# Where the first modulation of a layer is computed: at the head of the layer, or beside the mixers of the layer before

## The chip, the cores and the metric

The kernel runs on one core of a Trainium2 chip. The metric is the device time of one execution in microseconds (us). Lower is better.

## The reference

One inference step of a two-layer decoder trunk, for 512 prompt tokens and 8 single-token samples with shared weights (520 columns in all, width 1024). Cut to what matters here:

```python
def _block(x, c, st, pos, lb, p):
    mod = silu(c) @ p['ada_w'] + p['ada_b']               # 6 x 1024 per sequence
    sh1, sc1, g1, sh2, sc2, g2 = split(mod, 6)
    h = _rmsnorm(x, p['norm_mix_w']) * (1.0 + sc1) + sh1  # the first modulation
    mix, new_st = _mixer(h, st, pos, lb, p)               # RWKV-7, retention, gated delta, HGRN2, gates, w_out
    x = x + g1 * mix
    h = _rmsnorm(x, p['norm_ffn_w']) * (1.0 + sc2) + sh2
    gu = h @ p['w_gate_up']
    x = x + g2 * ((silu(gu[..., :D_FF]) * gu[..., D_FF:]) @ p['w_down'])
    return x, new_st
# two layers, then y = _rmsnorm(x, final_norm_w)
```

`c` (the conditioning) is the same in both layers and does not depend on x. So `mod` of every layer could be computed at any time; only h needs x.

## The kernel before, in words

Everything lies transposed: features on the 128 partitions (`KT` = 8 tiles), the 520 tokens along the free axis. The program has three parts: a block that loads constants and x and prepares tables, a hardware loop over the two layers (`nc.Fori`, L460), and a last block with the final norm. Between them all engines meet at a barrier, and the loop jumps back at its end. Inside a layer, each engine has its own instruction list, and semaphores tie them together.

**Weights.** They come as tiles of 128 x 1024 (0.5 MB) through a ring of four slots. `loads()` sets the order, SP issues a load as soon as the slot's last user is done (`load_tile`, L548). Since TensorE multiplies here in three parts (high x high, high x low, low x high), each weight tile of a large product is split first: the high part by ScalarE (`round_weights`, L1162) or by GpSimd (L602), the low part by GpSimd in two halves (L605). A large product (`large`, L652) is 48 matmuls of 128 x 260, six for each of eight slices of the input. It writes one of the two banks `gm`, which ScalarE or VectorE must empty before the product after next may start.

**Modulation.** The 48 tiles of `mod` come in twelve groups of four (`ADA_STEP`). A group is two products `ada` (L684, each from two ring tiles, taken by ScalarE at L1148 into a room of the arena) and one `turn` (L699), which turns the result onto the partitions with `PICK`; VectorE adds the bias (`modulation`, L2017). Groups 0 to 3 hold shift and scale of the first norm. Before the change they are the head of each layer: `first_modulation()` (L143).

**The order of a layer.** PE: wait for parameters and squares, sum over features (`feature_sums`, L756), the first modulation (L1074), then the plan. VectorE: squares of x and their sum (L2047 to L2051), modulation, `norm` (L1543), which also scales by 1 + sc. ScalarE: half of the squares, the root (`root_mean_square`, L1150: Ln, then Exp), the copies, its part of the norm.

**The plan** (`plan_layer`, L105) lists mixer stages and tasks. The mixers are HG, RW, GD, RT, one after the other, each a chain of steps of VectorE, ScalarE and small TensorE products. Beside each mixer stand tasks: projections of the next mixer, gates of the one before (two products each), and modulation groups, by `PARTS_BESIDE`. They are dealt out by the idle weights of the stages in `IDLE`. In a wait, TensorE takes up to 30 matmuls of the next task (`fill`, L730); a task that stands in front of a stage in the plan must be finished first (`finish`, L741). After the mixers come the out products, the second norm, 44 gate and up products and the 176 slices of the down product, each followed by `residual` (L2026).

Of the kernel before, what the change touches and what calls it, by code (L numbers as in the profile page):

```python
# [90 lines left out]
PARTS_BESIDE = {HG: 4, RW: 2, GD: 0, RT: 2}  # L91
# [13 lines left out]
def plan_layer():  # L105
# [8 lines left out]
    def with_modulation(n, tasks):  # L114


        m = N_ADA_FIRST + ADA_STEP * sum(PARTS_BESIDE[x] for x in range(n))
        first = len(tasks) - 2 * PARTS_BESIDE[n]
        out = tasks[:first]
        for i in range(first, len(tasks), 2):  # L120
            out += [("ada", n, m), tasks[i], ("ada", n, m + ADA_TILES), tasks[i + 1], ("turn", n, m)]
            m += ADA_STEP
        return out

    assert N_ADA_FIRST + sum(PARTS_BESIDE.values()) * ADA_STEP == N_ADA
# [17 lines left out]
def first_modulation():  # L143

    out = []
    for m in range(0, N_ADA_FIRST, 2 * ADA_STEP):
        out += [("ada", m + j) for j in range(0, 2 * ADA_STEP, ADA_TILES)]
        out += [("turn", m), ("turn", m + ADA_STEP)]
    return out


def wall_tiles():

    tiles = [("ada", m) for m in range(N_ADA_FIRST)]
    for kind, n, m in plan_layer():
        if kind == "ada":
# [6 lines left out]


N_WALL = len(wall_tiles())


def loads():


    tiles = wall_tiles()
    order = list(range(N_WALL))
    for i in range(ADA_TILES, N_WALL):
        if tiles[i][0] != "ada" and tiles[i - 1][0] == "ada":
            at = order.index(i)
            order[at - ADA_TILES:at + 1] = [i] + order[at - ADA_TILES:at]
# [25 lines left out]
def build(nc, xt, wall, wbranch, wsmall, params, lora, cond, consts, masks, rope, rettab, logits, fnorm, shift,  # L202
# [3 lines left out]
    with ctx:  # L206
# [164 lines left out]
        for name in ["weights_used", "wb_loaded0", "wb_loaded1", "gemm_done", "evac0", "evac1", "gate_used", "gate_ready",  # L371
# [3 lines left out]
                     "hi_made", "pool_step", "scores_zeroed", "parts_ready", "beta_split", "x_saved"] + [f"x_loaded{i}" for i in range(KT // 2)  # L375
# [15 lines left out]
        hi_made, pool_step, parts_ready, beta_split = s["hi_made"], s["pool_step"], s["parts_ready"], s["beta_split"]  # L391
        x_saved, x_loaded = s["x_saved"], [s[f"x_loaded{i}"] for i in range(KT // 2)]
# [3 lines left out]
        init_loaded, init_step, init_act, final_add, final_act, final_sq, final_sum, final_rs, final_y, y_stored = (  # L396
            ctx.enter_context(nc.semaphore(n)) for n in
            ("init_loaded", "init_step", "init_act", "final_add", "final_act", "final_sq", "final_sum", "final_rs",
             "final_y", "y_stored"))
# [7 lines left out]
        MKF = SCF[:, 0:(LEVELS + 1) * P128].rearrange("p (l i) -> p l i", l=LEVELS + 1)  # L407
        with nc.Block() as blk:
            @blk.sync
            def _(sp):  # L410
                for dst, src in ((X[:, :, :], xt), (CN[:, :], consts), (MKF, masks), (CI, cond),
                                 (LG, logits), (FN[:, :], fnorm)):
                    sp.dma_start(dst, src).then_inc(init_loaded, 16)
                sp.wait_ge(init_loaded, 96)

            @blk.vector
            def _(dve):
# [5 lines left out]
                dve.wait_ge(init_loaded, 96)  # L423
                step(dve.tensor_copy(MK[0:BLK, 0, :], MKF[0:BLK, LEVELS, 0:BLK]))

# [22 lines left out]
                step(dve.memset(CS[:, :], 0.0))  # L448
                step(dve.tensor_tensor(CSK, CI, CG, ALU.mult))
                step(dve.tensor_reduce(PICK[:, :], cst("ident").rearrange("p (c n) -> p n c", c=4)[:, 0:NMOD, :], AX_X, ALU.add))  # L450

            @blk.scalar
            def _(act):
                act.wait_ge(init_loaded, 96)
                act.activation(CG, CI, ACT.Sigmoid).then_inc(init_act, 1)
                act.wait_ge(init_step, 2 * DEPTH + 1)
                act.activation(LE, LE, ACT.Exp).then_inc(init_act, 1)
        nc.all_engine_barrier()

        with nc.Fori(0, DEPTH) as layer:  # L460
# [6 lines left out]


# [5 lines left out]
            for kind, _ in first_modulation():  # L474
                large_count += 1
                if kind == "ada":
                    last_use += within(ADA_TILES - 1) + [(gemm_done, large_count)]
                    shared += ADA_TILES - 1
            for kind, n, m in plan:
# [8 lines left out]
                if kind == "gate":  # L488
                    large_count += 1
                    if m % 2:  # L490
                        wb_last.append(large_count)
            for _ in range(KT + 2 * FT):
# [11 lines left out]
            splits = [(i, kind) for i, (kind, _) in enumerate(wall_tiles()) if kind != "ada"]  # L504
            consumer, at = [-1] * N_ADA_FIRST, []
# [14 lines left out]
            products, pool_sums = len(first_modulation()), {}  # L520
# [14 lines left out]
            def _(sp):  # L535
                for dst, src in ((PR[:, :], of_layer(params).rearrange("l p n -> (l p) n")),
                                 (LO[:, :, :], of_layer(lora).rearrange("l p k n -> (l p) k n")),
                                 (wsm[:, :, :], of_layer(wsmall).rearrange("l p k n -> (l p) k n")),
                                 (SHI[:, :, :], of_layer(shift).rearrange("l p k n -> (l p) k n")),
                                 (CVI[:, :, :, :], of_layer(convst).rearrange("l p k j n -> (l p) k j n"))):  # L540
                    sp.dma_start(dst, src).then_inc(small_loaded, 16)

                wall_l = of_layer(wall).rearrange("l n p k m -> (l n) p k m")
                wb_l = of_layer(wbranch).rearrange("l n p j k m -> (l n) p j k m")
# [1763 lines left out]
```

## Time and profile before

| | |
|---|---|
| median of 3 runs | 2802.61 us (2799.86 to 2806.51) |
| profiled execution, its own time | 2819.19 us |
| its span | 2817.4 us |
| TensorE busy in the span | 2343.8 us (83%) |
| mean granted TensorE clock | 0.891 of full |

The span runs from the first to the last instruction of the profiled execution. Busy times are unions per engine; TensorE's matmuls are pipelined, so its busy time is no measure of its peak. The profiled execution is 0.6% above the median.

### The profile page before, as it was taken

How to read it: one execution, taken by the hardware profiler on the slowest of the kernel's cores; microseconds unless marked ns; L12 is line 12 of the kernel's file. 1: busy time of each engine (PE TensorE's matmuls, PEld its weight loads, DVE VectorE, ACT ScalarE, POOL GpSimd, SP SyncE). 2: the span in 40 equal slices, each digit the busy share in tenths (PEclk: the TensorE clock that was granted, in tenths of full speed). 3: DMA queues.
4: the chain of work that ended last, by engine and by line, in shares of the span. 5: the costliest groups of instructions: out<-in, count | busy, mean ns of one | idle time of the engine just before them, and what ended most of it. 6: DMA issues, size and time to landing. Idle time of an engine off the chain costs nothing. (4 is left out here: it accounts for less than half of the span.)

```text
span 2817.4 us, 45798 instructions
## 1 busy us (share of the span) xinstructions
PE 2343.8 (83%) x19764; PEld 2153.5 (76%) x19764; DVE 1106.9 (39%) x1527; ACT 733.3 (26%) x907; POOL 832.1 (30%) x598
## 2 busy tenths in 40 slices
PE   4878787778889979999958778776878998999996
PEld 1866676567777979999928667665767788899996
DVE  1172575546343542221121644644644445322212
ACT  2342320231122232221124323113212133322211
POOL 1321220123132434444413212101412234344442
PEclk8978896788899989999969889887978999999998
DMA  5432121111123323222253211210202233232231
GB/s 195 135 106 69 49 70 49 46 41 43 63 92 99 110 68 90 90 91 90 68 193 108 101 65 56 70 61 28 61 31 84 90 99 106 75 91 91 84 97 62
DMA packets 68037, 233.45 MB, mean 83 GB/s; under 512 B 10736, under 2 KB 11248, under 8 KB 67312
## 3 DMA queue, kind: packets, MB, share of 16 engines
q1 hardware_dynamic: 60912, 214.88, 23.9%
q10 hardware_dynamic: 6912, 15.53, 1.6%
q8 instruction: 158, 2.59, 0.4%
q14 instruction: 55, 0.45, 0.1%
HBM read 219.03 MB, written 11.35 MB: 82 GB/s over the span
## 5 line engine op out<-in xcount | busy, mean ns | idle before, releaser
L605 POOL TENSOR_TENSOR ring_lo<-ring,w_hi 128x512 fp32r<-128x512 f32 x552 | 767.4, 1411 | 1512.8 <-ACT w_hi L1170 1446.1
L646 PE MATMUL gm<-H_hi,ring_lo 128*128 128x260 f32 x3456 | 754.0, 301 | 132.3 <-ACT GT L1414 34.7
L646 PE MATMUL gm<-H_hi,w_hi 128*128 128x260 f32 x3456 | 727.3, 293 | 0.9 <-ACT arena L1195 0.9
L646 PE MATMUL gm<-H_lo,w_hi 128*128 128x260 f32 x3456 | 724.2, 292 | 0.0
L646 PEld LDWEIGHTS gm<-H_hi,ring_lo 128*128 128x128 f32 x3456 | 567.3, 199 | 176.6 <-issue 116.2
L646 PEld LDWEIGHTS gm<-H_hi,w_hi 128*128 128x128 f32 x3456 | 558.9, 197 | 4.0 <-issue 2.0
L646 PEld LDWEIGHTS gm<-H_lo,w_hi 128*128 128x128 f32 x3456 | 559.8, 198 | 0.5 <-issue 0.5
L1170 ACT ACTIVATE w_hi<-ring 128x1024 fp32r<-128x1024 f32 x272 | 287.1, 1056 | 479.1 <-PE gm L646 214.6
L1107 PE MATMUL gm<-AF_hi,ring_lo 128*128 128x260 f32 x704 | 142.9, 284 | 6.4 <-DVE AF_lo L2095 6.4
L595 POOL TENSOR_TENSOR X<-X,GT 128x520 f32<-128x520 f32 x32 | 49.8, 1555 | 322.5 <-DVE GT L2075 322.5
L1107 PE MATMUL gm<-AF_hi,w_hi 128*128 128x260 f32 x704 | 142.2, 283 | 0.0
L1107 PE MATMUL gm<-AF_lo,w_hi 128*128 128x260 f32 x704 | 142.0, 283 | 0.0
L2030 DVE TENSOR_SCALAR Y<-gm,MOD 128x520 f32<-128x520 f32 x32 | 24.3, 759 | 273.8 <-PE gm L1107 232.1
L1414 ACT ACTIVATE GT<-gm 128x520 f32<-128x520 f32 x64 | 38.6, 603 | 347.0 <-PE gm L646 319.8
L2100 DVE TENSOR_TENSOR AT<-gm,GT 128x520 f32<-128x520 f32 x44 | 30.8, 700 | 247.0 <-ACT GT L1446 247.0
L678 PE MATMUL gm<-Y,WB 128*128 128x260 f32 x512 | 123.1, 383 | 1.1 <-ACT arena L1195 1.1
L1107 PEld LDWEIGHTS gm<-AF_hi,ring_lo 128*128 128x128 f32 x704 | 109.1, 189 | 6.8 <-DVE AF_lo L2095 6.8
L692 PE MATMUL gm<-ring,CS 128*32 128x512 f32 x384 | 80.1, 797 | 35.6 <-DMA ring<-wall 15.0
L1107 PEld LDWEIGHTS gm<-AF_lo,w_hi 128*128 128x128 f32 x704 | 109.4, 189 | 0.0
L1107 PEld LDWEIGHTS gm<-AF_hi,w_hi 128*128 128x128 f32 x704 | 109.0, 189 | 0.0
L678 PEld LDWEIGHTS gm<-Y,WB 128*128 128x128 f32 x512 | 92.9, 190 | 12.8 <-ACT arena L1195 1.4
L1405 ACT ACTIVATE PJ<-gm 128x520 f32<-128x520 f32 x64 | 38.6, 604 | 233.5 <-PE gm L646 167.6
(396 smaller groups left out, 2686.3 us busy)
## 6 DMA issues: line engine op xcount, KB each, us to landing
ring<-wall SPq DMA_DIRECT2D x372, 512.0 KB, 3.6
WB<-wbranch SPq DMA_DIRECT2D x32, 256.0 KB, 3.7
xsave<-X SPq DMA_DIRECT2D x2, 2080.0 KB, 10.4
X<-xsave ACTq DMA_DIRECT2D x8, 520.0 KB, 5.2
arena<-states ACTq DMA_DIRECT2D x8, 512.0 KB, 3.5
sst<-arena ACTq DMA_DIRECT2D x8, 512.0 KB, 3.7
X<-xt SPq DMA_DIRECT2D x1, 2080.0 KB, 7.7
y<-H SPq DMA_DIRECT2D x1, 2080.0 KB, 6.3
```

Of the source, the lines that this page charges most:

```text
L595: pool.tensor_tensor(MG[:, m, :], MG[:, m, :], GT[:, :], ALU.add).then_inc(gate_used, 1)
L605: pool.tensor_tensor(ring_lo[:, SLOT[i], k], ring[:, SLOT[i], k], hi[:, k].bitcast(F32), ALU.subtract).then_inc(parts_ready, 1)
L646: ins = pe.matmul(out[:, hf, 0:HALF], w[a][:, k, :], src[b][:, k, HALF * hf:HALF * (hf + 1)], start=first and a == "lo", stop=last and a == b)
L678: ins = pe.matmul(out[:, hf, 0:HALF], WB[:, m // 2 % 2, m % 2, k, :], Y[:, k, HALF * hf:HALF * (hf + 1)], start=k == 0, stop=k == 1)
L692: ins = pe.matmul(out[c:c + QUARTER, 0, :], CS[:, NMOD * (k0 + k + j):NMOD * (k0 + k + j) + QUARTER], w[:, j, :], start=True, stop=True)
L1107: ins = pe.matmul(out[:, hf, 0:HALF], w[a][:, i % 8, :], AF_parts[b][:, f, HALF * hf:HALF * (hf + 1)], start=f == 0 and a == "lo", stop=f ...
L1170: act.activation(w_hi[:, j % 2], ring[:, SLOT[splits[j][0]]], ACT.Copy).then_inc(hi_made, 1)
L1405: act.activation(h2(PJ[:, n % 2, m, :]), src, ACT.Copy).then_inc(done, 1)
L1414: act.activation(h2(GT[:, :]), src, ACT.Sigmoid).then_inc(done, 1)
L2030: step(ts(h2(WR), src, MOD[:, at + m, 0:1], None, MUL))
L2100: taken(tt(h2(AT[:, f % 2, :]), src, h2(GT[:, :]), MUL), done)
```

## The change

- The first layer's first modulation goes into the block in front of the loop, together with the squares of x, the root and the scale.
- Inside the loop, groups 0 to 3 stand beside the mixers and are computed for the coming layer (`of_coming`; in the last layer this is the first one's again). `PARTS_BESIDE` goes from 4, 2, 0, 2 to 4, 3, 3, 2. Their bias is added later, in front of the down product's residuals, when the coming layer's parameters are there.
- PR, LO, SHI and CVI of the coming layer are loaded in the feed-forward part. `wsm` is loaded behind the second projection tile.
- The squares of x for the next norm are made tile by tile behind the down product's residuals, and the feature sums and the root stand at the end of the layer. The final norm uses the same root, and y is stored in four parts.

```diff
-PARTS_BESIDE = {HG: 4, RW: 2, GD: 0, RT: 2}
+PARTS_BESIDE = {HG: 4, RW: 3, GD: 3, RT: 2}
+GROUPS = list(range(N_ADA_FIRST, N_ADA, ADA_STEP)) + list(range(0, N_ADA_FIRST, ADA_STEP))
...
     for m in range(0, N_ADA_FIRST, ADA_TILES):
+        out.append(("ada", m))
+        if m and m % ADA_STEP == 0:
+            out.append(("turn", m - ADA_STEP))
+    return out + [("turn", N_ADA_FIRST - ADA_STEP)]
...
         with nc.Block() as blk:
             @blk.sync
             def _(sp):
+                for dst, src in ((CI, cond), (CN[:, :], consts)):
+                    sp.dma_start(dst, src).then_inc(cond_loaded, 16)
+                for i in range(N_ADA_FIRST):
+                    if i == RING:
+                        sp.dma_start(X[:, :, :], xt).then_inc(x_read, 16)
+                        for dst, src in ((PR[:, :], params[0]), (MKF, masks), (LG, logits), (FN[:, :], fnorm),
+                                         (LO[:, :, :], lora[0]), (SHI[:, :, :], shift[0]),
+                                         (CVI[:, :, :, :], convst[0])):
+                            sp.dma_start(dst, src).then_inc(init_loaded, 16)
+                    if i >= RING:
+                        sp.wait_ge(*first_use[i - RING])
+                    sp.dma_start(ring[:, i % RING], wall[0, TILE["ada", i]]).then_inc(ring_full[i % RING], 16)
...
+                a = MOD[:, KT:2 * KT, :]
+                step(dve.scalar_tensor_tensor(a, a, 1.0, par("norm_mix", 0, KT).unsqueeze(2).to_broadcast([P128, KT, NMOD]),
+                                              ALU.add, ALU.mult))
...
-        nc.all_engine_barrier()
+        nc.all_engine_barrier(sems_to_clear=range(nums[0], nums[-1] + 1))
...
             @blk.sync
             def _(sp):
-                for dst, src in ((PR[:, :], of_layer(params).rearrange("l p n -> (l p) n")),
...
-                    sp.dma_start(dst, src).then_inc(small_loaded, 16)
...
+                        tile = TILE[USES[x]]
+                        sp.dma_start(ring[:, SLOT[x]], (wall_coming if tile < N_ADA_FIRST else wall_l)[tile]
+                                     ).then_inc(ring_full[SLOT[x]], 16)
...
+                    if USES[i] == ("gu", 2 * RING):
+                        sp.wait_ge(gemm_done, first_inner)
+                        for dst, src in ((PR[:, :], of_coming(params).rearrange("l p n -> (l p) n")),
...
+                            sp.dma_start(dst, src).then_inc(coming_loaded, 16)
...
             @blk.tensor
-                pe.wait_ge(small_loaded, 80)
-                pe.wait_ge(operands_v, count.next(operands_v))
-                feature_sums()
-                for kind, m in first_modulation():
-                    for _ in ada(m) if kind == "ada" else turn(AD_FIRST, m):
-                        pass
                 finish()
...
+                pe.wait_ge(operands_v, count.next(operands_v))
+                feature_sums()
...
             @blk.scalar
-                act.wait_ge(small_loaded, 80)
+                norm(0)
                 step(act.activation(NA[:, :], par("a_log")[0:4], ACT.Exp), for_vector)
-                step(act.activation(H[:, 4:, :], X[:, 4:, :], ACT.Square), for_vector)
-                root_mean_square()
-                for kind, m in first_modulation():
-                    take_modulation(AD_FIRST, m) if kind == "ada" else skip()
-                norm(0)
...
+                left = [(8 * (j - len(splits) + FT - 1), -1) for j in range(rounded[0], len(splits))]
+                for _, m in sorted(left + [(FT * (m + 1) + 4, m) for m in range(KT)]):
+                    if m < 0:
+                        round_weights()
+                    else:
+                        g[0] += 1
+                        taken_by_vector(g[0])
+                        step(act.activation(H[:, m, :], X[:, m, :], ACT.Square), for_vector)
+                root_mean_square()
...
             @blk.vector
+                dve.wait_ge(coming_loaded, 64)
+                step(tt(MOD[:, 0:N_ADA_FIRST, :], MOD[:, 0:N_ADA_FIRST, :], par("ada_b", 0, N_ADA_FIRST).unsqueeze(2)
+                        .to_broadcast([P128, N_ADA_FIRST, NMOD]), ADD))
+                scaled("norm_mix", KT)
                 for m in range(KT):
                     residual(m, 5 * KT)
+                    if m:
+                        from_scalar()
+                    if m > 1:
+                        add_square(m - 1)
+                from_scalar()
+                add_square(KT - 1, operands_v)
...
+                for k in range(0, KT, 2):
+                    sp.wait_ge(final_y, k + 2)
+                    sp.dma_start(y_out[:, k:k + 2, :], H[:, k:k + 2, :]).then_inc(y_stored, 16)
```

How this moves instructions is seen best on TensorE. The head of its list before; `ring,CS` are the modulation products, `PICK` the turns, `H,CN` the feature sums, `H_hi,ring_lo` the first large product, and all of it is inside the loop:

```order
L609 UNCONDITIONAL_BRANCH
L759 MATMUL mx<-H,CN 128x260 x2
L692 MATMUL gm<-ring,CS 32x512 x16
L705 MATMUL gm<-PICK,arena 128x9 x16
L692 MATMUL gm<-ring,CS 32x512 x16
L705 MATMUL gm<-PICK,arena 128x9 x16
L646 MATMUL gm<-H_hi,ring_lo 128x260 x2
```

The same place of the changed kernel:

```order
L467 MATMUL gm<-ring,CS 32x512 x12
L475 MATMUL gm<-PICK,arena 128x9 x8
L467 MATMUL gm<-ring,CS 32x512 x8
L475 MATMUL gm<-PICK,arena 128x9 x8
L467 MATMUL gm<-ring,CS 32x512 x8
L482 MATMUL mx<-H,CN 128x260 x2
L475 MATMUL gm<-PICK,arena 128x9 x8
L467 MATMUL gm<-ring,CS 32x512 x4
L475 MATMUL gm<-PICK,arena 128x9 x8
L433 UNCONDITIONAL_BRANCH
L570 UNCONDITIONAL_BRANCH
L729 UNCONDITIONAL_BRANCH
```

The modulation stands in front of the loop (L570), each turn one product later than its operands, and the loop's own list begins with the large product.

The second place is TensorE in the mixer GD, between the inverse of the first pair of chunks (`arena 64x64`) and the first chunk. Before:

```order
L848 MATMUL mx<-arena 64x64 x8
L852 MATMUL mx<-arena 64x64 x8
L646 MATMUL gm<-H_hi,w_hi 128x260
L646 MATMUL gm<-H_hi,ring_lo 128x260 x2
L646 MATMUL gm<-H_lo,w_hi 128x260 x2
```

And in the changed kernel:

```order
L968 MATMUL mx<-arena 64x64 x8
L972 MATMUL mx<-arena 64x64 x8
L812 MATMUL gm<-ring,CS 32x512 x4
L987 MATMUL mx<-S,arena 128x64 x4
L766 MATMUL gm<-H_hi,ring_lo 128x260 x2
```

A modulation product stands where a large product was, and the chunk's own product comes directly behind it; six such products and three turns are new in GD, two and one in RW.

## Rows read from the trace of the kernel before

**Rows 1.** The page, part 1: busy time, share of the span, instructions.

```profile
PE 2343.8 (83%) x19764; PEld 2153.5 (76%) x19764; DVE 1106.9 (39%) x1527; ACT 733.3 (26%) x907; POOL 832.1 (30%) x598
```

**Rows 2.** Timeline of the head (start us, us, engine, line, operation; idle before, releaser).

```profile
11.97 0.26 ACT L455 ACTIVATE arena<-arena 128x72 f32<-128x72 f32 x1 [9.94 <-DMA FN<-fnorm]
...
17.98 0.22 DVE L450 TENSOR_REDUCE PICK<-CN 128x9 f32<-128x36 f32 x1
...
19.28 0.35 SPq L541 DMA_DIRECT2D PR<-params  x1
...
36.33 3.64 PE L692 MATMUL gm<-ring,CS 128*32 128x512 f32 x16
...
49.20 7.00 PE L705 MATMUL gm<-PICK,arena 128*128 128x9 f32 x32
...
75.08 0.22 DVE L1548 TENSOR_TENSOR H<-X,GT 128x64 f32<-128x64 f32 x1
...
78.59 0.77 PE L646 MATMUL gm<-H_hi,ring_lo 128*128 128x260 f32 x2 [4.11 <-DVE H_lo L1558]
...
87.14 1.64 DVE L1558 SCALAR_TENSOR_TENSOR H_lo<-H,MOD,H_hi 128x512 fp32r<-128x512 f32 x2
...
89.64 0.41 PE L646 MATMUL gm<-H_hi,ring_lo 128*128 128x260 f32 x2
```

**Rows 3.** Timeline between the two layers.

```profile
1408.90 0.70 DVE L2032 TENSOR_TENSOR X<-X,Y 128x520 f32<-128x520 f32 x1
...
1414.89 0.34 SPq L541 DMA_DIRECT2D PR<-params  x1
...
1430.11 2.07 PE L759 MATMUL mx<-H,CN 128*128 128x260 f32 x4 [22.30 <-DVE H L2036]
...
1432.26 1.28 ACT L1135 ACT_TABLE_LOAD   x1 [9.13 <-PE mx L759]
...
1435.57 0.64 ACT L1136 ACTIVATE GT<-GT 128x520 f32<-128x520 f32 x1
...
1457.78 1.89 POOL L602 TENSOR_TENSOR w_hi<-ring,CN 128x1024 fp32r<-128x1024 f32 x1 [34.37 <-DMA ring<-wall]
...
1459.75 2.48 POOL L605 TENSOR_TENSOR ring_lo<-ring,w_hi 128x512 fp32r<-128x512 f32 x2
...
1473.24 0.77 PE L646 MATMUL gm<-H_hi,ring_lo 128*128 128x260 f32 x2 [4.12 <-DVE H_lo L1558]
```

**Rows 4.** Timeline of the end.

```profile
2791.19 0.70 DVE L2032 TENSOR_TENSOR X<-X,Y 128x520 f32<-128x520 f32 x1
2793.52 2.33 DVE L2116 TENSOR_TENSOR H<-X 128x2080 f32<-128x2080 f32 x1 [1.63 <-PEq L2110]
...
2805.16 5.46 DVE L2126 SCALAR_TENSOR_TENSOR H<-X,FN,GT 128x520 f32<-128x520 f32 x8 [4.87 <-ACT GT L2144]
...
2810.64 0.35 SPq L2149 DMA_DIRECT2D y<-H  x1
```

**Rows 5.** DMA issues, 19 to 80 us and whole span (KB, median us to landing).

```profile
ring<-wall SPq DMA_DIRECT2D x20, 512.0 KB, 4.9
...
X<-xsave ACTq DMA_DIRECT2D x8, 520.0 KB, 5.2
```

**Rows 6.** Stretches: length, busy us (count) by engine, granted clock, DMA share, GB/s.

```profile
131.00:297.00 166.00, 126.04 (x1612) 108.10 (x1609) 84.62 (x112) 58.52 (x68) 32.85 (x22) 0.79 0.28 94
297.00:597.00 300.00, 227.12 (x1757) 200.17 (x1757) 153.37 (x236) 74.20 (x94) 43.15 (x31) 0.81 0.17 53
597.00:820.00 223.00, 180.43 (x1549) 165.43 (x1548) 112.43 (x167) 48.09 (x61) 64.52 (x46) 0.87 0.18 57
```

**Rows 7.** Timeline: a modulation product and two turns beside the mixer RT.

```profile
828.63 1.06 PE L692 MATMUL gm<-ring,CS 128*32 128x512 f32 x8
...
853.78 1.85 PE L705 MATMUL gm<-PICK,arena 128*128 128x9 f32 x16
...
890.82 3.58 PE L705 MATMUL gm<-PICK,arena 128*128 128x9 f32 x16 [3.13 <-ACT GT L1414]
```

More of the change, by code:

```diff
@@ L114, in with_modulation @@
     def with_modulation(n, tasks):
-        m = N_ADA_FIRST + ADA_STEP * sum(PARTS_BESIDE[x] for x in range(n))
+        group = sum(PARTS_BESIDE[x] for x in range(n))
         first = len(tasks) - 2 * PARTS_BESIDE[n]
@@ L145, in first_modulation @@
     out = []
[L146 to L149, printed above, removed]
+    for m in range(0, N_ADA_FIRST, ADA_TILES):
+        out.append(("ada", m))
+        if m and m % ADA_STEP == 0:
+            out.append(("turn", m - ADA_STEP))
+    return out + [("turn", N_ADA_FIRST - ADA_STEP)]
 def wall_tiles():
@@ L155, in wall_tiles @@
     for kind, n, m in plan_layer():
[L156 removed]
+        if kind == "ada" and m >= N_ADA_FIRST:
             tiles += [("ada", m + j) for j in range(ADA_TILES)]
@@ L162, in wall_tiles, with wall_uses @@
     return tiles + [("down", i) for i in range(FT)]
+def wall_uses():
+    uses = []
+    for kind, n, m in plan_layer():
+        if kind == "ada":
+            uses += [("ada", m + j) for j in range(ADA_TILES)]
+        if kind in ("proj", "gate"):
+            uses.append((kind, n * 8 + m))
+    return uses + wall_tiles()[len(uses):]
 N_WALL = len(wall_tiles())
+TILE = {x: i for i, x in enumerate(wall_tiles())}
+USES = wall_uses()
+assert sorted(USES) == sorted(TILE)
 def loads():
-    tiles = wall_tiles()
     order = list(range(N_WALL))
     for i in range(ADA_TILES, N_WALL):
-        if tiles[i][0] != "ada" and tiles[i - 1][0] == "ada":
+        if USES[i][0] != "ada" and USES[i - 1][0] == "ada":
             at = order.index(i)
@@ L407, in build @@
         MKF = SCF[:, 0:(LEVELS + 1) * P128].rearrange("p (l i) -> p l i", l=LEVELS + 1)
+        first = first_modulation()
+        first_use, product, shared = [], 0, 0
+        for kind, _ in first:
+            product += 1
+            if kind == "ada":
+                shared += 1
+                first_use += [(weights_used, shared), (gemm_done, product)]
+        sums_after = first.index(("ada", N_ADA_FIRST - 2 * ADA_TILES))
         with nc.Block() as blk:
@@ L582, in _, with split @@
                 zero = cst("zero").unsqueeze(2).to_broadcast([P128, 8, P128])
+                def split(j):
+                    i = splits[j][0]
+                    wait_for_tile(pool, j)
+                    hi = w_hi[:, j % 2]
+                    made = len([x for x in on_scalar if x <= j])
+                    if j in on_scalar:
+                        pool.wait_ge(hi_made, made)
+                    else:
+                        pool.tensor_tensor(hi, ring[:, SLOT[i]], zero, ALU.add).then_inc(pool_step, 1)
+                        pool.wait_ge(pool_step, j + 1 - made)
+                    for k in (slice(0, 4), slice(4, 8)):
+                        pool.tensor_tensor(ring_lo[:, SLOT[i], k], ring[:, SLOT[i], k], hi[:, k].bitcast(F32), ALU.subtract
+                                           ).then_inc(parts_ready, 1)
                 pool.memset(SCF[:, 0:2048], 0.0).then_inc(scores_zeroed, 1)
-                pool.wait_ge(small_loaded, 80)
+                first_tiles = 2
+                for j in range(first_tiles):
+                    split(j)
+                pool.wait_ge(small_loaded, 16)
                 pool.tensor_tensor(wsm_hi[:, :, :], wsm[:, :, :], zero[:, :, 0:64], ALU.add).then_inc(beta_split, 1)
```

211 lines of the change are left out of this document (118 added, 93 removed).

## The prediction

> **What bounds the kernel now.** I read the page first: TensorE's busy time against the span, then the timeline of three short stretches (the head of the program, the turn from one layer to the next, the end), and last the table of stretches inside a layer. The page gives TensorE 2343.8 us of a span of 2817.4 [rows 1], so the engine is busy five sixths of the time, and the question is where the other 470 us are. The timeline shows two places at which it is almost only fed with small work. At the head, the first large product starts at 78.59 and the second at 89.64 [rows 2]. Between the layers, the last residual add ends at 1408.90 + 0.70 = 1409.60 and the first large product of the next layer starts at 1473.24: 63.6 us in which squares, their sum, the root, sixteen modulation tiles and four turns run one behind the other [rows 3]. At the end, 25.5 us pass between the last residual add (2791.89) and the end of the span [rows 4]. The reader should see that these three are chains with nothing beside them, so what is taken out of them comes off the time in full. The stretches beside the mixers are different: in 297 to 597 TensorE is busy 227.12 us of 300, in 597 to 820 it is 180.43 of 223 [rows 6]. There the mixer's chain of VectorE and ScalarE steps and the large products fill each other's gaps, and neither is alone the bound.
>
> **The turn between the layers.** After the change the squares of tiles 0 to 6 are made while the down products run (VectorE has little else there), so from 1409.60 only two adds are left, 0.70 each like the residual's add [rows 3], then the sum over features 2.07, then logarithm and exponential with their table loads: from 1432.18 to 1435.57 + 0.64 = 1436.21, that is 4.0 [rows 3]. Together 7.5. The way through the end of the block and back to SP's first issue stays: 1414.89 - 1409.60 = 5.3 [rows 3]. So the new block starts at 1422.4. Now the first weight tile is what comes last, no longer the modulation: landing 4.9 [rows 5], GpSimd's rounding 1.89, half of its 2.48 for the first low part [rows 3]: first product at 8.05 behind the block's start. The normalization runs beside it; VectorE's part took 75.08 to 88.78, 13.7 us [rows 2], and the product needs its last tile. Eight slices of six matmuls at the half rate of a cool engine would take some 11 us, so I put the second product 17 us behind the block's start: 1439.4. Before it was 11.05 behind the first [rows 2], at 1484.3. **Gain 44.9.** The second modulation's scale and the small parameter loads go beside the out and feed-forward products, where each large product needs one tile of 0.5 MB and the ring is four deep: cost nothing while that cover stands; 0.5 MB of parameters would cost at most one tile's landing, 4.9, if it did not.
>
> Here a rule speaks against the size of this. The row shows a table load of 1.28 at 1432.26 and the next load of the chain ending just in front of 1435.57; the whole root takes 4.0 [rows 3]. The Trainium skill, page ScalarE: Activation LUTs, section What ACT_TABLE_LOAD costs, says that a switch costs the load of about 1283 ns and a drain of about 1380 ns besides. By it the root would take some 2.8 more, at this place and at the end, where it is newly alone on the path; an estimate by the page would be 5.6 us less gain. The trace does not show that drain, and the sum goes by the trace.
>
> **The head.** The block in front of the loop loads conditioning and constants (0.7 MB), four tiles, then x and the parameters (3.2 MB), then twelve tiles as the ring comes free. Before, 3.35 MB were there at 11.97 after issues from 0.74 [rows 2], about 0.33 MB/us, so the fifth tile lands no earlier than about 20. Eight tiles went through TensorE between 36.33 and 49.20, 1.6 each [rows 2]: twelve more take 19. Behind the last one stand a turn of 3.5 (7.00 for two at half rate [rows 2]) and, an estimate, 1 for ScalarE's copy and VectorE's last steps; and the turns, the feature sums and VectorE's squares that now lie between the tiles I put at another 5 to 6. That is 49. SP's first issue in the loop was 1.1 behind the end of the first block (18.20 to 19.28 [rows 2]); then the second product 17 later, at 67.1 instead of 89.64. **Gain 22.5**; the terms that I guess (the 5 to 6, the entry) leave it between 15 and 28.
>
> **The end.** Two adds, sum and root 7.5, the loop's exit 1.6 [rows 4], eight products 5.46, the issue and the last quarter's landing: 5.2 for 520 KB in [rows 5], say 5. Together 19.6 against 25.5 [rows 4]. **Gain 5.9.**
>
> **What it costs.** Every layer now carries four groups more beside RW, GD, and (shifted) RT, and the second layer carries them for nothing, since it makes the first layer's modulation again: eight groups. A group is two products of four tiles' halves, 1.06 each, and a turn of 1.85 at full rate [rows 7], 4.0 of TensorE, with two copies on ScalarE and one small step on VectorE, each in the mixer's own order. From below: all of it falls into the idle 73 us of 297 to 597 and the idle 43 of 597 to 820 [rows 6], cost 0; a gain is excluded, as nothing leaves the mixers. From above: in 131 to 297, where four groups stand, TensorE idles 40 us, 10 per group [rows 6], and a group would cost 14. Between them lies the turn that waited 3.13 for ScalarE's activation [rows 7]. I take TensorE's own time, 8 x 4.0 = **32 us**: the new stretches are busy for three quarters and more, which is nearer to full than to empty, and what the idle parts swallow the copies in ScalarE's queue give back. The projections of GD and RT also move forward in their stretches (all eight RW gates before stage 5 of GD instead of stage 9); I cost that at nothing, as the same work is done between the same two ends.
>
> **Sum.** 44.9 + 22.5 + 5.9 = 73.3 gained, 32 lost: 41.3. From the profiled execution's 2819.19 that gives 2777.9. The median of the runs is 2802.61, lower by the factor 0.9941, so I predict 2762.
>
> **Rivals.** *The groups are hidden.* For it: 116 idle us in two stretches of one layer; against: a ring of four tiles that a group takes half of. Cost 10, time 2740. *Each new group also brings a wait.* ScalarE and VectorE serve banks in the order of their program, so TensorE stands until a mixer step is through; 3.1 a group as at 890.82 [rows 7] makes 57 instead of 32, time 2786. *The front block takes as long as the head did*, because x, parameters and tiles share the queues and the turns run at half rate: no gain of 22.5, time 2784. *Slower than before:* every one of the eight groups costs 14 like those beside HG, because a modulation product holds one of the two banks until ScalarE comes to it, and the large product behind it cannot start; 112 lost against 73 gained, time 2841. It decides from 9.2 us per group on. Against it: part of HG's idle time belongs to its own chain and not to the groups. That the change does nothing of what it says I can rule out nearly: the order of instructions shows the moved products.
>
> **Numbers.** Forecast 0.53 (its own range 2746 to 2777), hidden 0.18, waits 0.16, front block 0.06, slower 0.05, the rest near no change 0.02. About 0.2% is what a measurement of this kernel tells from no change. Faster 0.93, same 0.02, slower 0.05. The range goes from the hidden case to a little over the cases of waits: 2740 to 2792.
>
> **What would show it.** Right: the first large product near 58 and the second near 67; the step from the last residual add of layer one to the next layer's second product near 30 instead of 75; four table loads less exposed but each root still 4.0; the end near 20 behind the last residual add. The cost shows as the length from the second large product of a layer to its first out product, up by about 16 in each. Wrong: if that length grows by over 35, with TensorE waiting for ScalarE's copies or for ring tiles in front of modulation products, or if the second layer's first product waits for a landing behind the store of x.

## The result, and the profile after the change

The change makes the kernel slower: 2826.05 us (median of 5 runs, 2823.9 to 2837.28) against 2806.51 for the kernel before in the same comparison (median of 5, 2799.86 to 2811.22). The ratio is 1.0069, with a 95% interval of 1.004 to 1.0098. The forecast was 2762, range 2740 to 2792, and "slower" had a chance of 5 in 100.

The profiled execution of the changed kernel took 2837.28 us, its span is 2835.5; 18.1 us more than the span before. Page, part 1, against [rows 1]:

```profile
PE 2390.3 (84%) x19892; PEld 2198.2 (78%) x19892; DVE 1125.7 (40%) x1540; ACT 741.9 (26%) x927; POOL 844.3 (30%) x598
```

TensorE is busy for 46.5 us more. That is more than the added work explains: the change moves work and adds only one layer's wasted modulation, four groups of 4.0 us.

Timeline of the head, against [rows 2]:

```profile
56.09 0.80 PE L766 MATMUL gm<-H_hi,ring_lo 128*128 128x260 f32 x2 [9.52 <-POOL ring_lo L708]
...
67.91 0.80 PE L766 MATMUL gm<-H_hi,ring_lo 128*128 128x260 f32 x2 [0.80 <-DVE H_lo L1677]
...
72.25 0.64 PE L766 MATMUL gm<-H_hi,ring_lo 128*128 128x260 f32 x2
```

A row of this kind opens each of the eight slices of a large product. 67.91 is the sixth slice of the first product, which waited for VectorE; the ninth row, 72.25, is the start of the second product.

Timeline between the layers, against [rows 3]:

```profile
1421.83 0.70 DVE L2155 TENSOR_TENSOR X<-X,Y 128x520 f32<-128x520 f32 x1
...
1424.06 1.15 PE L879 MATMUL mx<-H,CN 128*128 128x260 f32 x4 [3.33 <-DVE H L2159]
1425.28 1.28 ACT L1251 ACT_TABLE_LOAD   x1 [2.08 <-PE mx L879]
1426.58 0.69 ACT L1251 ACTIVATE GT<-mx,CN 128x520 f32<-128x520 f32 x1
1427.29 1.28 ACT L1252 ACT_TABLE_LOAD   x1
1428.58 0.64 ACT L1252 ACTIVATE GT<-GT 128x520 f32<-128x520 f32 x1
...
1434.47 1.29 SPq L659 DMA_DIRECT2D ring<-wall  x2
...
1442.86 0.80 PE L766 MATMUL gm<-H_hi,ring_lo 128*128 128x260 f32 x2 [17.66 <-POOL ring_lo L708]
...
1444.46 2.34 POOL L705 TENSOR_TENSOR w_hi<-ring,CN 128x1024 fp32r<-128x1024 f32 x1
1445.08 2.27 DVE L1677 SCALAR_TENSOR_TENSOR H_lo<-H,MOD,H_hi 128x512 fp32r<-128x512 f32 x1
...
1458.24 0.64 PE L766 MATMUL gm<-H_hi,ring_lo 128*128 128x260 f32 x2
```

The last row is the ninth again, the start of the layer's second product. The same step of VectorE in the kernel before, with GpSimd idle:

```profile
1475.49 0.75 DVE L1558 SCALAR_TENSOR_TENSOR H_lo<-H,MOD,H_hi 128x512 fp32r<-128x512 f32 x1
```

Timeline of the end, against [rows 4]:

```profile
2817.28 0.70 DVE L2155 TENSOR_TENSOR X<-X,Y 128x520 f32<-128x520 f32 x1
...
2826.92 5.46 DVE L2241 SCALAR_TENSOR_TENSOR H<-X,FN,GT 128x520 f32<-128x520 f32 x8 [7.46 <-PEq L2234]
2828.37 4.36 SPq L2248 DMA_DIRECT2D y<-H  x4
```

So all three places got shorter, by 63 us in all where 73 were forecast. The loss is inside the layer. The table cuts the span at the first instruction of each mixer (the clearing of its state on VectorE), at the first out product and at the last down product:

| stretch | before | after | | 
|---|---|---|---|
| start to HG, layer 1 | 131.0 | 114.3 | -16.7 |
| HG (layer 1, 2) | 152.5, 150.6 | 149.2, 151.6 | -2.3 |
| RW | 275.3, 267.0 | 287.4, 291.8 | **+36.9** |
| GD | 229.0, 226.9 | 249.9, 249.9 | **+43.9** |
| RT with the last gates | 168.9, 167.3 | 167.3, 170.1 | +1.2 |
| out, gate and up, down | 451.1, 452.6 | 452.6, 452.6 | +1.5 |
| end of down 1 to HG of layer 2 | 117.9 | 79.6 | -38.3 |
| end of down 2 to the end | 27.3 | 19.3 | -8.0 |

63.0 us were gained outside the mixers; 81.2 were lost, nearly all beside RW and GD. Table of stretches RW, GD, RW, GD (two layers), first of the kernel before, then of the changed one (columns: stretch and length, busy us of PE, PEld, DVE, ACT, POOL with counts, granted clock, DMA share, GB/s):

```profile
283.50:558.80 275.30, 205.45 (x1659) 181.80 (x1660) 156.09 (x238) 60.44 (x82) 45.08 (x32) 0.81 0.18 55
558.80:787.90 229.10, 180.05 (x1508) 163.69 (x1506) 107.64 (x165) 61.25 (x73) 57.64 (x40) 0.85 0.16 52
1676.30:1943.30 267.00, 198.19 (x1659) 176.69 (x1660) 155.28 (x238) 60.46 (x82) 47.73 (x32) 0.85 0.18 57
1943.30:2170.20 226.90, 177.88 (x1508) 161.65 (x1506) 107.65 (x165) 61.25 (x73) 57.68 (x40) 0.85 0.17 52
```

```profile
263.50:550.90 287.40, 217.35 (x1691) 192.73 (x1692) 155.44 (x239) 62.21 (x84) 49.22 (x32) 0.80 0.19 60
550.90:800.80 249.90, 199.01 (x1604) 175.31 (x1602) 109.48 (x167) 64.94 (x79) 57.28 (x40) 0.84 0.22 73
1651.80:1943.60 291.80, 221.58 (x1691) 196.86 (x1692) 154.42 (x240) 62.12 (x84) 51.09 (x32) 0.78 0.18 59
1943.60:2193.50 249.90, 199.03 (x1604) 175.29 (x1602) 109.43 (x167) 64.90 (x79) 57.23 (x40) 0.84 0.23 73
```

The reader should see three things. VectorE's work is nearly unchanged (155 and 109 us where it was 156 and 108), so the mixers did not get more to do. TensorE's idle time (length less PE busy) is about the same, 69.9 and 68.8 before and 70.1 and 70.2 after beside RW, 49.0 before and 50.9 after beside GD: **on balance nothing of it was filled**. And TensorE's busy time grew by 11.9 and 23.4 beside RW, 19.0 and 21.2 beside GD, together 75.4, where eight groups hold 32 (two of them stand beside RW, six beside GD). The matmul and clock records split this. I take the busy time and subtract half of the part that ran at the lower granted clock (1.2 GHz); that is the work at the full rate (2.4 GHz). It grew by 31.2 us in the four stretches, just the forecast's 32. The part that ran at the lower clock grew from 207.4 to 296.0 us, and half of that growth, 44 us, is time lost to the clock.

After this comparison I had three theories. **A**: the large products stand elsewhere. `plan_layer` deals the tasks out by their number; with small modulation tasks added, the projections and gates slide forward (all RW gates due ahead of GD's stage 5 instead of 10). This costs the time. **B**: the groups themselves cost 10 us each, by banks, copies and waits. **C**: more small products lower the clock, wherever the large ones stand. Theory D came after the first four runs: a group costs TensorE's own time.

### The profile page after: what moved, and what is told of

Its sections match the earlier page's. It is cut to its first block and busy times, and to the rows that moved or that the text cites. A ratio compares the mean times of both kernels' runs of the same rounds, so it can differ in the third digit from the quotient of the medians.

```text
span 2835.5 us, 46135 instructions
## 1 busy us (share of the span) xinstructions
PE 2390.3 (84%) x19892; PEld 2198.2 (78%) x19892; DVE 1125.7 (40%) x1540; ACT 741.9 (26%) x927; POOL 844.3 (30%) x598
## 5 line engine op out<-in xcount | busy, mean ns | idle before, releaser
L708 POOL TENSOR_TENSOR ring_lo<-ring,w_hi 128x512 fp32r<-128x512 f32 x552 | 781.3, 1436 | 1561.2 <-ACT w_hi L1286 1509.1
L766 PE MATMUL gm<-H_hi,ring_lo 128*128 128x260 f32 x3456 | 762.9, 303 | 147.1 <-POOL ring_lo L708 48.2
L766 PE MATMUL gm<-H_lo,w_hi 128*128 128x260 f32 x3456 | 733.6, 295 | 1.9 <-ACT arena L1311 1.9
L766 PEld LDWEIGHTS gm<-H_hi,ring_lo 128*128 128x128 f32 x3456 | 573.5, 201 | 196.6 <-issue 117.8
L766 PEld LDWEIGHTS gm<-H_lo,w_hi 128*128 128x128 f32 x3456 | 567.4, 200 | 3.3 <-ACT arena L1311 2.7
L2187 DVE TENSOR_TENSOR GT<-gm,GT 128x520 f32<-128x520 f32 x48 | 33.6, 699 | 184.7 <-PE gm L798 148.9
L798 PEld LDWEIGHTS gm<-Y,WB 128*128 128x128 f32 x512 | 92.6, 190 | 12.9 <-DMA WB<-wbranch 1.6
```

Source lines behind the costliest of these rows:

```text
L708: pool.tensor_tensor(ring_lo[:, SLOT[i], k], ring[:, SLOT[i], k], hi[:, k].bitcast(F32), ALU.subtract).then_inc(parts_ready, 1)
L766: ins = pe.matmul(out[:, hf, 0:HALF], w[a][:, k, :], src[b][:, k, HALF * hf:HALF * (hf + 1)], start=first and a == "lo", stop=last and a == b)
L798: ins = pe.matmul(out[:, hf, 0:HALF], WB[:, m // 2 % 2, m % 2, k, :], Y[:, k, HALF * hf:HALF * (hf + 1)], start=k == 0, stop=k == 1)
L2187: taken(tt(h2(GT[:, :]), src, h2(GT[:, :]), MUL), done)
```

## The experiments

All of them change `plan_layer`, the plan or one product, and all are compared with the kernel before on the same chip. Two runs are set against each other by their ratios to it; 0.01 in the ratio is 28 us. In a plan's table each string below is one mixer; each word is a stage, L the next large product (projection, gate, beta), a and t the next modulation product and turn.

### e1 to e4: the places and the groups apart

**e1**, the changed kernel with the large products at their old due places:

```diff
+GIVEN = {RW: "L L L LL L LL L L La L a L t a L - a - L - t - - a L a - L t -",
+         GD: "L L L L L a L L a L t L a L a L t L a - L a L L Lt -"}
...
+            if n in GIVEN:
+                plan += [(large if x == "L" else small)[n].pop(0) for x in GIVEN[n].split()[i] if x != "-"]
```

> The changed kernel, but with the large products (projections, gates, beta) beside RW and GD due at the stages at which they stood before the change; the six groups of modulation beside them stand between. Theory A (where the large products stand is what cost the time: taken out of the later stages of RW and GD, which then run at the lower granted clock): RW and GD together shorter than in the changed kernel by some 22 us per layer, time near 2782. Theory B (the groups themselves cost 10 us each, by waits for banks, copies and ring tiles, wherever the large products stand): as the changed kernel, 2826 +- 6. Theory C (the clock falls because more small products are in these stretches, not because of the order): also 2826, with the same busy time at the lower clock in RW and GD as in the changed kernel.

Measured: 2805.49 us, ratio 0.9959 (0.9941 to 0.9977). With the same work as the changed kernel, due at other stages, it is 1.1% faster, some 31 us.

**e2**, the kernel before with the new due places and nothing else:

```diff
+GIVEN = {RW: "L L LL LL L LL L L - L - L a - - - La - - - Lt - - a - La - L t -",
+         GD: "LL LL L LL L L L - L - - L - - - L - L - - - - L L - -"}
```

> The kernel before, with no group added and nothing else changed, but the large products beside RW and GD due at the stages of the changed kernel. Theory A: slower than before by about the 44 us that the comparison of the traces puts on the lower clock, near 2850. Theories B and C: no change, 2806 +- 6.

Measured: 2831.53 us, ratio 1.0061 (1.0042 to 1.0081): 17 us slower than before, without one added instruction. The waits of VectorE and of TensorE beside GD show how. Before:

```profile
PE gm L646 <- ACT GT L1414: 17.3, 3, 9.5
...
DVE GT L2075 <- ACT GT L1414: 6.1, 2, 4.4
```

and in e2 (columns: engine, tile and line, what it waited for; us, times, longest):

```profile
DVE GT L2084 <- PE gm L687: 22.1, 4, 9.7
```

```profile
PE gm L655 <- ACT GT L1423: 15.1, 3, 9.8
PE mx L800 <- DVE arena L1974: 11.4, 2, 10.2
...
PE mx L925 <- DVE arena L1713: 6.4, 1, 6.4
```

Two gates are now due ahead of one stage, three times among the first four. VectorE, which carries the mixer's chain, stands in front of each gate's product (22.1 us). Later, where the products were taken away, TensorE waits for the mixer with nothing beside it, 10.2 us in one piece. GD takes 239.7 us instead of 229.0 and 226.9, with the same work at full rate (156.6 against 156.9) and an idle time of 58.7 instead of 49.0: here the loss is idle time.

**e3**, the changed kernel with the eight extra groups where no mixer runs:

```diff
-PARTS_BESIDE = {HG: 4, RW: 3, GD: 3, RT: 2}
+PARTS_BESIDE = {HG: 4, RW: 2, GD: 0, RT: 2}
...
-    plan = project(HG)
+    plan = between(HG, project(HG), GROUPS[:2])
...
-    return plan + gates(RT)
+    return plan + between(RT, gates(RT), GROUPS[-2:])
```

> The changed kernel with RW and GD exactly as before the change (two groups beside RW, none beside GD), and the four extra groups of a layer in the dense stretches without a mixer: two between the eight HG projections, two between the eight last gates. All theories: RW and GD back at their lengths before. A group costs 4.0 us of TensorE at full rate there, or up to the landing of its four tiles; with 4 to 6 us a group 32 to 48 us in all against the 63 us gained outside the mixers: 2775 to 2791. If the ring of tiles is what bounds these stretches (six tiles for two large products and a group), the two stretches grow by over 14 us each and the time is 2800 or more.

Measured: 2791.98 us, ratio 0.992 (0.9892 to 0.9948). RW is back at 274.0 and 274.9, GD at 229.0 and 228.3. The projections' stretch grew by 9.8 and 12.3 us against the changed kernel for two groups, the last gates' by 9.5 and 7.4: 4 to 6 us a group. That puts this run just above its forecast of 2775 to 2791. The ring did not bound it.

**e4**, dealing by TensorE time:

```diff
+LOAD = {"proj": 6, "gate": 7.5, "beta": 6, "ada": 1, "turn": 2}
...
+            weights = [LOAD[x[0]] if n in (RW, GD) else 1 for x in tasks]
```

> The changed kernel, but the tasks beside RW and GD are dealt out by their TensorE time (projection 6, gate 7.5, modulation product 1, turn 2) instead of by count, so that the large products are spread over the stages again, the last ones later than even before the change. Theory A: 2782 or below. Theories B and C: 2826 +- 6.

Measured: 2807.92 us, ratio 0.9977 (0.9964 to 0.999). A general rule gives back nearly what the copied table of e1 does (26 us against the changed kernel, e1 31).

What follows from the four. Places alone cost 17 us; with the groups in, the places cost 31. So A is right in kind, but the full 44 of e1's and e2's forecast did not come: neither 2782 nor 2850. B and C, which wanted no difference at all, are out as the whole cause; that added groups lower the clock, the core of C, does show beside GD in the table below. In e1 only 11.5 us are won (0.41%) of the 63 gained outside the mixers, so its eight groups cost 51, that is 6.4 each. The lower clock is not the places' alone either. TensorE's time at the lower clock, us of layer 1 and 2:

| | RW | GD |
|---|---|---|
| before | 67.7, 51.8 | 46.2, 41.7 |
| e2, new places, no group | 81.5, 71.4 | 49.0, 48.7 |
| e1, old places, groups | 72.9, 69.9 | 64.5, 73.6 |
| changed kernel | 83.5, 93.0 | 59.8, 59.7 |

Beside GD the groups raise it, beside RW both do.

### e5 to e8: what a group costs, and where

**e5**, seven of twelve groups where no mixer runs (the plan's two ends take them by `with_modulation`, with `START, END = 3, 4`):

```diff
-PARTS_BESIDE = {HG: 4, RW: 3, GD: 3, RT: 2}
+PARTS_BESIDE = {HG: 1, RW: 2, GD: 0, RT: 2}
+START, END = 3, 4
```

> As e3, but seven groups of a layer in the dense stretches (three between the HG projections, four between the last gates), one beside HG (instead of four), two beside RW, none beside GD, two beside RT. Theory D (a group costs its TensorE time, 4 to 5 us, in either kind of stretch, since nothing of the mixers' idle time is filled by it): as e3, 2792 +- 6, HG's stretch shorter by 3 x 5 = 15 and the dense stretches longer by as much. Theory B (beside a mixer a group costs some 10 us): the six groups moved save 5 us each, about 2762; HG's stretch falls by 30. Theory E (groups beside HG are largely hidden in its 34 idle us): HG falls by less than 8, time 2800 to 2810.

Measured: **2771.87 us, ratio 0.9862** (0.9841 to 0.9882), the fastest of all and faster than both kernels. HG fell from 143.4 and 144.0 (e3) to 125.3 and 122.9 for three groups, 6 to 7 each; the last gates' stretch grew by 10.3 and 9.7 for two, 5 each. Between theories D and B, nearer B for HG. But a shorter list is dealt out anew: HG's projections stand at other stages in e5 than in e3, so the 6 to 7 hold the groups and the places together.

**e6**, RW's two groups moved beside RT (`{HG: 4, RW: 0, GD: 0, RT: 4}`, `START, END = 2, 2`):

> As e3 (two and two groups in the dense stretches, four beside HG), but the two groups beside RW stand beside RT (four there, none beside RW and GD). Theory D: as e3, 2792 +- 6; RW shorter by 8 and RT longer by 8. If a group costs more beside RW, where TensorE runs for a third at the lower clock, than beside RT (granted clock 0.95, 12 us idle): RW falls by more than 12 a layer, RT grows by 8 to 10, time 2780 to 2786.

Measured: 2853.47 us, ratio 1.0157 (1.0134 to 1.018), the slowest of all and outside every forecast. RT with the last gates grew by 24 us a layer against e3 for two groups: in layer 1 by 10.0 of work at full rate, 8.0 of idle time and 6.3 by the lower clock. TensorE waited there 1.6 us for tiles of the gates' small weights (`WB`) and never for a tile of the ring, so the ring does not bound it; the gates beside RT were dealt out anew as well, and no run separates that from the groups. And RW, which had lost 7.2 us of work, grew from 274.0 and 274.9 to 285.3 and 285.3.

**e7**, both moves (`{HG: 1, RW: 0, GD: 0, RT: 4}`, `START, END = 3, 4`):

> Both moves together: seven groups in the dense stretches, one beside HG, none beside RW and GD, four beside RT. Theory D: 2792 +- 8. If groups beside the mixers HG and RW cost more than 4 to 5 us each: the sum of the two effects, down to some 2755. If the RT stretch with eight more tiles and the dense stretches are bounded by the ring: 2800 or more.

Measured: 2834.67 us, ratio 1.0079 (1.0063 to 1.0095): 22 us below e6, as e5 is 16 below e3; within the intervals the two effects add. The time lies above the 2800 of the third case, but its reason, the ring, is not what e6 shows.

**e8**, the changed kernel with GD's groups thinned on TensorE alone (it leaves out part of the modulation):

```diff
-                        for j in range(2):
+                        for j in range(n == GD, 2):
...
-                    for j in range(ADA_STEP):
+                    for j in range(3 * (n == GD), ADA_STEP):
```

> The changed kernel with the three groups beside GD thinned on TensorE alone: half of each modulation product's matmuls (2 of 4) and a quarter of each turn's (2 of 8) are left, with all waits, loads, copies and banks as before. It leaves out part of the modulation that these groups compute. A group loses 1.06 + 0.75 x 1.85 = 2.4 us at full rate. Theory D (TensorE's own time is what a group costs): GD shorter by 7 to 10 us in each layer, time 2826 - 17 = 2809. Theory B (banks, copies and waits are what it costs): GD unchanged, 2826 +- 6.

Measured: 2812.26 us, ratio 1.0006 (0.9989 to 1.0024), about 18 us below the changed kernel. Table of stretches, RW and GD of layer 1:

```profile
264.70:546.40 281.70, 211.45 (x1691) 188.38 (x1692) 154.99 (x239) 62.22 (x84) 49.04 (x32) 0.82 0.19 61
546.40:785.70 239.30, 185.57 (x1544) 162.29 (x1542) 108.72 (x168) 64.93 (x79) 57.28 (x40) 0.87 0.23 76
```

GD takes 239.3 instead of 249.9, which is e2's GD without any group (239.7). All waits for banks, copies and ring tiles were still there and cost nothing against e2. So the bank is out, and the price lies on TensorE. It is not its time at full rate, though. The thinning took only 3.1 us of such work out of three groups (169.1 to 166.0; my 2.4 a group was too high), and the thinned groups still hold 9.4 us more than e2 has (156.6), for nothing in length. TensorE's time at the lower clock fell from 59.8 to 39.0 us, worth 10.4, while the idle time rose by 2.8. So the clock pays for more than the work does. Against e2 the thin groups even spent less at the lower clock (39.0 against 49.0 us). Why they kept the clock up is open.

### e9 to e12: which stretch, and the limit

**e9** and **e10** are the changed kernel with e1's table for RW alone and for GD alone.

> The changed kernel with the old due places of the large products beside RW alone; those beside GD stay where the change put them. By the stage lengths of e1 against the changed kernel (RW 280 against 287 to 292, GD 250 in both) the places matter beside RW once the groups are there: nearly the time of e1, 2806 to 2812. If the places beside GD matter as they did without groups (e2: GD +11 a layer), 2826 minus half of the 20: 2816 or more.

> The other half: the old due places beside GD alone, RW as the change has it. By the stage lengths: as the changed kernel, 2820 to 2828, GD at 250. If the places beside GD decide: 2805 to 2812 with GD under 242.

Measured: e9 2807.42 us, ratio 0.9979 (0.9958 to 0.9999); e10 2817.09 us, ratio 1.001 (0.9988 to 1.0031). Against the changed kernel's 1.0069 the old places beside RW give back 0.9%, 25 us, those beside GD 0.6%, 17 us, both together (e1) 31. They do not add up, but with intervals of 5 us and more on each that is no contradiction. RW matters more, as expected. Whether GD's places matter once the groups are there stays open. The medians say 17 us where at most 6 were expected; but of the 17.6 us between the profiled executions of e10 and the changed kernel only 2.8 lie beside GD (248.4 and 248.6 against 249.9 twice), and 6.5 lie beside RW, where the two plans are the same. In the profile of e9 RW gives back 19.9 us. One plan beside RW took 275.3 and 267.0 in the two layers of one execution, so a few us in one stretch prove nothing.

**e11**, e6 with the old due places beside RW, still without a group there:

```diff
+GIVEN = {RW: "L L L LL L LL L L L - L - - L - - - L - - - - - L - - L - -"}
...
+            if n in GIVEN:
+                now = given + GIVEN[n].split()[i].count("L")
```

> As e6 (no group beside RW), but the large products beside RW due where they stood before the change. In e6 they were dealt out anew because the list was shorter, and RW grew by 11 us a layer though 8 us of TensorE work had left it. If the due places alone did that: RW at 274 - 8 to 14 = 260 to 266, and the time some 40 below e6, 2808 to 2818. If the groups of modulation in the list have nothing to do with it and RW's chain got longer for another reason: RW still at 285, time 2853.

Measured: 2815.82 us, ratio 1.001 (0.9985 to 1.0034), 38 us below e6, 41 by the ratios. RW takes 266.8 and 260.2 instead of 285.3 twice. The waits of TensorE beside RW, first e6 (layer 1), then e11 (layer 2; layer 1 differs only in the last row, 6.5 instead of 7.5):

```profile
PE gm L768 <- POOL ring_lo L710: 14.0, 3, 7.1
PE mx L913 <- DVE arena L2000: 13.0, 1, 13.0
PE mx L900 <- DVE arena L1987: 12.6, 1, 12.6
PE gm L768 <- ACT GT L1527: 9.7, 3, 6.9
```

```profile
PE mx L917 <- DVE arena L2004: 13.4, 1, 13.4
PE gm L772 <- POOL ring_lo L714: 10.5, 2, 7.1
PE mx L893 <- DVE arena L2036: 7.5, 1, 7.5
```

The 13.0 at L913 is the 13.4 at L917, the same step in both. The 12.6 at L900 stands in e6 alone. There TensorE waits for VectorE's step and has nothing to fill with. By the code `fill` may run ahead of the plan by two products only (`may_start`), and in e6 the products are due later, so these two were done. In e11, where they are due earlier, this wait is not in the list. Then in e6 the last HG gate, due one stage later than in e11 and close behind two others, holds up the end of RW (timeline, VectorE):

```profile
529.42 1.24 DVE L2017 TENSOR_TENSOR arena<-arena 128x1040 f32<-128x1040 f32 x1
540.57 0.70 DVE L2186 TENSOR_TENSOR X<-gm,GT 128x520 f32<-128x520 f32 x1 [9.91 <-ACT GT L1527]
```

VectorE stands for 9.9 us in front of the gate's step with the mixer's steps behind it. So the dealing alone did both, as the expectation's first case had it.

**e12**, e5 with HG's last group and the first RW projection also ahead of HG (a part of its edit, against e5):

```diff
-    plan = with_modulation(HG, project(HG), START, 0)
+    plan = project(HG)[:1] + with_modulation(HG, project(HG)[1:] + project(RW)[:1], START, 0)
```

> As e5, but none beside HG: four groups between the first projections, two beside RW, two beside RT, four between the last gates. A group cost 6.5 to 7 us beside HG (e5 against e3) and 4 to 5 in the dense stretch: 2 us a layer less than e5, 2766 to 2772. If the first projection of RW, which is now due ahead of HG's first stage, or the projections of RW dealt out anew cost HG a wait: HG over 120 us and 2772 to 2785.

Measured: 2803.42 us, ratio 0.996 (0.9942 to 0.9977), 28 us slower than e5 and outside both of its forecasts. HG in e5, then in e12:

```profile
125.20:250.50 125.30, 95.95 (x1470) 85.08 (x1468) 68.32 (x92) 49.55 (x56) 27.10 (x18) 0.89 0.23 72
```

```profile
143.70:266.00 122.30, 80.69 (x1344) 72.09 (x1343) 67.65 (x92) 47.12 (x52) 22.59 (x16) 0.84 0.15 48
```

TensorE's work in HG fell by 15 us at full rate (87.8 to 72.8; 5.4 of it moved on into RW), and HG became 3.0 shorter in layer 1 and 0.9 in layer 2. The stretch ahead of it grew by 13.8 and 17.3. I read this as the other bound: with little beside it, HG lasts some 122 us by its own chain, and what stands beside it up to there is free. With one group HG is just at that length, with four it is 18 to 21 us above. This is argued, not shown, since e12 has a rival: its RW projections stand at other stages, and TensorE waited in HG for GpSimd's low parts of them, 21.5 us in three pieces against 2.3 us in e5. What speaks for the chain is that VectorE's three largest waits are nearly the same in both (in sum 12.9, 9.5 and 9.1 us in e12; 11.2, 9.1 and 8.0 in e5).

## Why the prediction was wrong

**The gains came out ten short.** In the head the second product starts at 72.25 (forecast 67.1, [rows 2]): 17.4 gained for 22.5. Between the layers it starts at 1458.24, 35.7 behind the last residual add instead of 74.7: 39.0 gained for 44.9. Most terms held: adds, sum and root took 6.7 us from 1422.53 to 1429.22 (7.5), the jump to SP's first issue 5.3 (5.3), the first product came 8.4 behind it (8.05), and in the head SP's first issue came at 48.54 (50.1; the transfer rate of 0.33 MB/us in that sum is 0.30 by its own numbers, 3.35 MB from 0.74 to 11.97, and did no harm). The mis-sized term is the 17 us from SP's first issue to the second product; it was 23.7 in the head and 23.8 between the layers. I had let the normalization run beside the weights at its old 13.7 us. It took 21.9, from 1434.44 to 1456.30, since VectorE's steps of 0.75 us took 1.4 to 2.3 while GpSimd rounded and split the first tiles (1438.84 to 1453.29), and the first product's slices waited for them. Before the change the split was done (1466.84) when the normalization began (1469.73). The end gained 8.0 (5.9), since a quarter of y lands in 2.7 us and I had put 5. In the table of stretches 63.0 us arrived for a forecast of 73.3. That miss of ten is no change of sign.

**The table loads** behaved as in [rows 3]: a load of 1.28 at 1425.28, the activation at 1426.58, the next load at 1427.29. The drain of about 1380 ns that the Trainium skill, page ScalarE: Activation LUTs, section What ACT_TABLE_LOAD costs, adds to a switch is not there, although the root is newly alone on the path; both roots took 3.9.

**The step that failed is the cost, 32 for 81.** Three things were in it.

1. *"I cost that at nothing, as the same work is done between the same two ends."* This sentence on the projections and gates that move forward is the first thing that was wrong, and without its 31 us the change would have been faster (e1). It costs 17 us without the groups (e2) and 31 with them (e1 against the changed kernel). The view was there: [rows 6] show TensorE idle and VectorE with a chain of its own, which means that the order decides who waits. A due place is a wait of the chain (22.1 us of VectorE for gates beside GD), and an emptied stage is idle time that `fill` may not use. (The old place of the last RW gate is ahead of stage 10, not 9.)
2. *TensorE's own time, 4.0 a group.* As work this was exact: 31.2 us more at full rate. As time it was not. At the old places a group costs 6.4 (e1), since beside RW and GD much of what is added runs at the lower clock. I priced the turn and the product "at full rate" while [rows 6] give 0.81 and 0.87 as the granted clock of the very stretches.
3. *Filling.* I let the idle parts swallow what the copies cost. They swallowed little: at the old places (e1) the idle time of the four stretches fell by 7.1 us of 236.6. That it stayed at 70 and 50 in the changed kernel is two effects in one: set against e2, the groups filled 7.8 us in each layer beside GD, where the new places had opened 9.7, and added 6.8 beside RW. RW and GD had no room for more, since taking TensorE's work out made each of them shorter (e11, e8).

**The rivals.** "Hidden" is out. "The front block takes as long" is out too, as 17.4 us were gained there. "Each group brings a wait" gave 57 us of cost; e1 lands near it (51), but for another reason, since e8 kept the waits beside GD and lost the cost. "Slower than before" gave 14 a group from a bank held; the loss was 10 a group and above its threshold of 9.2, so the sign was this rival's, but its mechanism was not. The list of what would show me wrong asked for over 35 us more in a layer from second product to out; it was 28.8 in the first layer and 52.2 in the second, where 16 were forecast for each. It named the wrong waits: no new wait for copies or ring tiles appears in front of modulation products.

What stays open: what RT's 24 us in e6 are, whether GD's places matter once the groups are in, and above all why the granted clock falls by so much more than the added work beside RW and GD. No kernel here held the clock by itself.

## What to carry to other kernels

Where tasks are dealt out between the steps of a chain by their number, adding small tasks moves the large ones: compare the due place of each large task before and after, and cost it, since moving alone made 17 to 41 us here. Idle time of an engine beside a chain is hardly room: price an addition at no less than the engine's time at the clock that the stretch has, since the clock may fall further, and count it as free only while the stretch is no longer than its chain (for HG some 122 us, if e12 is read rightly). Small work that nobody waits for belongs where the engine runs dense (4 to 6 us a group between plain products, 6 to 7 beside a mixer): with seven of twelve groups there, the same change is 1.4% faster instead of 0.7% slower.

## What the runs showed of the hardware

Fewer matmuls can give more clock: with 60 fewer records of TensorE in three groups beside GD (1604 to 1544), the granted clock there rose from 0.84 to 0.87 and the time at the lower level fell by 20.8 us of 59.8, though TensorE was also idle 2.8 us longer. One plan can run at different clocks within one execution: before the change RW took 275.3 us at a granted clock of 0.81 in the first layer and 267.0 at 0.85 in the second, with the same instructions. And VectorE slowed down beside GpSimd: in the changed kernel its 128x512 normalization steps of 0.75 us took 1.41 to 2.27 us as long as GpSimd worked on the first weight tiles (1438.84 to 1453.29), and 0.75 again at 1453.88.
